# A fused two-block transformer kernel: weight slots with the low parts written in place, eight raw slots, and more modulation tiles on TensorE

## Chip, cores and metric

The kernel runs on one core of one Trainium2 chip. The metric is the device time of one execution in microseconds.

## What is computed

Two transformer blocks in a row, on 256 tokens of width 2048, all in float32. Cut to what matters here:

```
# block 1: adaptive norms, a Fourier mixer, an MLP of hidden width 8192
sh1, sc1, g1, sh2, sc2, g2 = split(silu(c) @ w_mod + b_mod, 6)     # w_mod: 2048 x 12288
h = rms_norm(x, g) * (1 + sc1) + sh1
y = real(fft2(h, tokens and groups of 256 features)) @ fnet_w_out
x = x + g1 * rms_norm(y);  x = x + g2 * rms_norm(relu(mod(x, sh2, sc2) @ w_mlp_in)**2 @ w_mlp_out)
# block 2: x -> w_in (12 groups of 512 columns: gated linear attention, forgetting attention,
#          attention to 256 memory tokens with keys and values mem @ w_mem_kv), gates, @ w_out
x = x + (o * gate) @ w_out;  x = x + relu(rms_norm(x) @ w_up)**2 @ w_down
```

All matrices are read once: 450 MB and more of weights in a run.

## The kernel before

The program is written out for each engine, with semaphores.

**Weights.** A weight chunk is 256 rows by 512 columns, 512 KB, in SBUF as 128 partitions by 1024 floats. A group is eight chunks (`CH`), 2048 rows of 512 columns. There are 688 chunks: 16 for the memory's keys and values (`G_MEM`), 32 for fnet_w_out (`G_FN`), 256 for each MLP, 96 for w_in (`G_WIN`), 32 for w_out. Float32 accuracy is reached with two fp32r parts: ScalarE copies `raw` to `wh` (high part, `hi`, L755), VectorE writes `wl = raw - wh` (low part, `lo`, L1054), and TensorE multiplies high by high, high by low and low by high. `wh` and `wl` have eight slots each, one for each chunk of a group; `raw` has four (`RAW`). `T_chunk` keeps weights stationary (L379 and L380 in the MLPs, L383 to L385 elsewhere), `N_chunk` the activations (L397 to L399).

**Modulation.** A modulation tile is 128 rows by 1024 columns of w_mod, also 512 KB and in the same `raw` slots. Each of the six vectors has 32. VectorE adds each tile, scaled by silu(c), into an accumulator (`gemv`, L1080, a chain along each half); the tiles in `PE_MOD` go to TensorE instead, as eight products with one column (`mod_chunk`, L436: 16 instructions in the trace). `mod_sum` (L448) then adds up the accumulator over partitions with more one-column products. The tiles of g2 use a slot of their own (`slot`), loaded by GpSimd's queue during the first MLP.

**Order.** All loads into `raw` are numbered in one line (`chunk_c`, `mod_c`), load cc goes to slot cc % RAW, and SyncE issues them in that order, each behind a wait that the slot's former content is used up: `raw_used`, incremented by `lo` for a weight chunk, by `gemv` or `mod_chunk` for a tile. The order is: 32 tiles of sc1; 16 chunks of w_mem_kv, each followed by two tiles of sh1; 32 tiles of g1 (while TensorE does the DFT); 32 chunks of fnet_w_out, each followed by a tile of sc2; 32 tiles of sh2; the first MLP; w_in; w_out; the second MLP.

Every engine runs its list in order. ScalarE's `hi` waits for the landing and for the multiplication of the chunk eight earlier (`chunk_used`), VectorE's `lo` for `hi`, TensorE for `lo`. On VectorE and ScalarE, `lo_run` and `hi_run` handle chunks 4 to 7 of a group and 0 to 3 of the next, and behind that stands the evacuation of the group's sums from PSUM (`ps`), in w_in also the steps of the attention: `lvl_post` and `lvl_pre` prepare a decay level (`qd`, `kd`, L1394), which TensorE multiplies in `att_level` (L626) between two chunks. In sh2, TensorE does tiles 3 and 5, then the transposes of the residual stream (L421, `SH2_TURN`), which wait for VectorE's `dg`, then the other tiles; the sums of its halves are the last thing before the MLP.

Of the kernel before, what the change touches and what calls it, by code (L numbers as in the profile page):

```python
# [34 lines left out]
P = 128  # L35
# [7 lines left out]
RAW = 4  # L43
# [5 lines left out]
PE_MOD = dict(sc1=(2, 8, 13, 18, 24), sh1=(), sc2=(), sh2=(3, 5, 20, 25))  # L49
# [12 lines left out]
def program(nc, x, c, w_mod, b_mod, norm_g, w_mlp_in, w_mlp_out, fnet_w_out, mem, attn_g, w_in, gla_w2, gla_b,  # L62
# [3 lines left out]
    with ctx:  # L66
# [10 lines left out]
        O_RAW, O_WH, O_WL = 0, 16 * KB, 48 * KB  # L77
# [17 lines left out]
        wl = at("wl", [P, CH, 2, GC], F32R, O_WL)  # L95
# [125 lines left out]
        def _(sp):  # L221
            def load(cc, view):

                s = cc % RAW
                if cc >= RAW:
                    sp.wait_ge(sem(f"raw_used{s}"), cc // RAW)
                sp.dma_start(raw_slot(s, view), view).then_inc(sem(f"raw_landed{s}"), 16)
# [30 lines left out]
            def ring_group(r0, view_of):  # L258

                for i in range(CH):  # L260
                    sp.wait_ge(sem(f"raw_used{i % RAW}"), r0 + i // RAW)
                    sp.dma_start(raw[:, i % RAW, :].rearrange("p (t n) -> p t n", t=2),
                                 view_of(i)).then_inc(sem(f"raw_landed{i % RAW}"), 16)

            def mlp_loads(G0, w1, w2_):
                r0 = (CH * G0 + C_OFF) // RAW
                with sp.Fori(0, QT) as q:
                    with sp.Fori(0, GQ) as g:
                        ring_group(r0 + 16 * q + 2 * g,
                                   lambda i: rows(w1)[:, 2 * i:2 * i + 2, bass.ds(q * D + g * GC, GC)])  # L270
                    with sp.Fori(0, GQ) as g:
                        ring_group(r0 + 8 + 16 * q + 2 * g,
                                   lambda i: rows(w2_)[:, bass.ds(q * KT + 2 * i, 2), bass.ds(g * GC, GC)])

            mlp_loads(G_ML1, w_mlp_in[0], w_mlp_out[0])
            for k, (name, off) in enumerate(WIN_GROUPS):
                ring_group((CH * (G_WIN + k) + C_OFF) // RAW,
                           lambda i: rows(w_in)[:, 2 * i:2 * i + 2, W_IN[name] + off:W_IN[name] + off + GC])
            with sp.Fori(0, GQ) as g:
                ring_group((CH * G_WO + C_OFF) // RAW + 2 * g,  # L280
                           lambda i: rows(w_out)[:, 2 * i:2 * i + 2, bass.ds(g * GC, GC)])
# [83 lines left out]
        def _(pe):  # L365
            mm = nc.tensor.matmul

            def T_chunk(G, i, wide, s, r):

                pe.wait_ge(sem(f"raw_used{s}"), r)  # L370
                par = G % 2
                for t in range(2):
                    kt = 2 * i + t
                    for j in range(4):
                        a, b = wh[:, i, t, j * P:(j + 1) * P], wl[:, i, t, j * P:(j + 1) * P]
# [12 lines left out]
            def N_chunk(G, i, act, wide, s, r):  # L388

                pe.wait_ge(sem(f"raw_used{s}"), r)  # L390
                par = G % 2
                for t in range(2):
                    kt = 2 * i + t
                    for half in range(HALVES):
                        o = ps[:, (4 if wide else 2) * par + half, :]
                        hi, lo = (act[:, kt, z, half * P:(half + 1) * P] for z in range(2))
                        mm(o, hi, wh[:, i, t, :], start=kt == 0, stop=False, skip_group_check=True)  # L397
                        mm(o, hi, wl[:, i, t, :], start=False, stop=False, skip_group_check=True)  # L398
                        last = mm(o, lo, wh[:, i, t, :], start=False, stop=kt == KT - 1, skip_group_check=True)  # L399
                last.then_inc(sem("chunk_used"), 1)  # L400
# [24 lines left out]

            for part in range(2):
                pe.wait_ge(sem(f"rows_in{part}"), 16 * ((N_ROWS + 1 - part) // 2))
            nc.tensor.transpose(ps[:, 0, 0:VROWS], vrow[0:VROWS, :], ident[0:VROWS, 0:VROWS]).then_inc(sem("vt_mm"), 1)

            def mod_chunk(vec, c0, n, bank, start=False):  # L430
# [7 lines left out]
                last.then_inc(sem(f"raw_used{s}"), 1)  # L438

            def mod_sum(vec, c0, a, bank, halves=(0, 1)):  # L440

                for half in halves:
                    n = [n for n in range(MODN) if mod_part(vec, n)[1] == half and n not in PE_MOD[vec]][-1]
                    s, r = slot_of(mod_c(c0, n))
                    pe.wait_ge(sem(f"raw_used{s}"), r)
# [14 lines left out]
            mod_sum("sc1", C_SC1, 0, 2)  # L460
            for i in range(CH):
                if i % 2 == 0:
                    pe.wait_ge(sem("xt_ready"), 1 + i // 2)
                T_chunk(G_MEM, i, False, *slot_of(chunk_c(i)))
            for i in range(CH):
                if i == 0:
                    pe.wait_ge(sem("mod_out"), 1)
                N_chunk(G_MEM + 1, i, xt, False, *slot_of(chunk_c(CH + i)))
# [53 lines left out]
            for n in (MODN - 2, MODN - 1):  # L522
                s, r = slot_of(mod_c(C_G1, n))
                pe.wait_ge(sem(f"raw_used{s}"), r)
            gate_rows(0, (4, 5, 6, 7))

            for g in range(GQ):
                bank_free(G_FN + g)
                for i in range(CH):
                    if g == 0:  # L530
                        pe.wait_ge(sem("fm_lo"), i + 1)
                    N_chunk(G_FN + g, i, xt, False, *slot_of(chunk_c(CH * (G_FN + g) + i)))
# [16 lines left out]
            def mlp(G0, build, ups, between=None):  # L549

                r0 = (CH * G0 + C_OFF) // RAW

                def down(q, p, e, last=False):
                    pe.wait_ge(sem("evacuated"), q * 8 + p * 2 + (G0 + 4 + e - 1))
                    for i in range(CH):
# [3 lines left out]
                        N_chunk(G0 + e, i, u, True, i % RAW, q * 16 + p * 4 + (r0 + 8 + 2 * e + i // RAW + 1))  # L559
# [3 lines left out]
                def quarter(q, last=False):  # L563
                    with pe.Fori(0, 2) as p:
                        for e in range(2):
                            pe.wait_ge(sem("evacuated"), q * 8 + p * 2 + (G0 + e - 1))
                            for i in range(CH):
                                if i % 2 == 0 and e == 0:
                                    pe.wait_ge(sem("xt_ready"), 4 * build + 1 + i // 2)
                                T_chunk(G0 + e, i, True, i % RAW, q * 16 + p * 4 + (r0 + 2 * e + i // RAW + 1))  # L570
# [109 lines left out]
            for k, (name, off) in enumerate(WIN_GROUPS):  # L680
                G = G_WIN + k
                bank_free(G)
                for i in range(CH):
                    if k == 0 and i % 2 == 0:
                        pe.wait_ge(sem("xt_ready"), 8 + i // 2 + 1)
                    sr = slot_of(CH * G + C_OFF + i)
# [41 lines left out]
            with pe.Fori(0, 2) as p:  # L728
                for e in range(2):
                    pe.wait_ge(sem("evacuated"), p * 2 + (G_WO + e - 1))  # L730
                    for i in range(CH):
                        if i % 2 == 0 and e == 0:
                            pe.wait_ge(sem("z_lo"), i // 2 + 1)
                        N_chunk(G_WO + e, i, u, False, i % RAW, p * 4 + ((CH * G_WO + C_OFF) // RAW + 2 * e + i // RAW + 1))
# [5 lines left out]
        def _(act):  # L740
# [20 lines left out]
            def hi_run(m0, between=None):  # L761

                for j in range(CH):
# [4 lines left out]
                    hi(i, (j % RAW, (m0 + (C_OFF + RAW * (j // RAW) + RAW)) * 4), m0 + (j - CH + 1))  # L768
# [128 lines left out]
            def mlp_quarter(G0, ups, q, last=False):  # L897
# [11 lines left out]
                def down(p, e, final=False):  # L909
                    m0 = q * 64 + p * 16 + (CH * (G0 + 4 + e) + 4)  # L910
                    if final:
                        for j in range(4):
                            hi(4 + j, (j % RAW, (m0 + (C_OFF + RAW)) * 4), m0 + (j - CH + 1))
# [127 lines left out]
        def _(dve):  # L1041
# [18 lines left out]
            def lo_run(m0, between=None):  # L1060
                for j in range(CH):
                    if between:
                        between(j)
                    lo((4 + j) % CH, j % RAW, m0 + (j + 1))
# [3 lines left out]
            def gemv(vec, c0, n, a):  # L1068
# [6 lines left out]
                if (vec, half) in summed:  # L1075
                    s0, r0 = summed[vec, half]
                    dve.wait_ge(sem(f"raw_used{s0}"), r0)
                summed[vec, half] = (s, r)
                t = (acc[0], acc[1], acc2)[a][:, half * MODC:(half + 1) * MODC]
                V.scalar_tensor_tensor(out=t, in0=raw[:, s, :], scalar=siluc[:, kt:kt + 1], in1=t,  # L1080
                                       op0=ALU.mult, op1=ALU.add).then_inc(sem(f"raw_used{s}"), 1)
# [197 lines left out]
            def mlp_quarter(G0, ups, q, side, onto, last=False):  # L1279
# [34 lines left out]
                def down(p, e, tail=False):  # L1314
# [4 lines left out]
                    if tail and not side:  # L1319
                        for j in range(4):  # L1320
                            lo(4 + j, j % RAW, m0 + (j + 1))
# [280 lines left out]
```

## Time and profile before

| | us |
|---|---|
| three timed runs | 2348.45 median (2344.02, 2348.45, 2353.89) |
| span of the profiled execution, first to last instruction | 2343.0 |
| TensorE (PE) busy | 2171.3 |
| VectorE (DVE) busy | 1401.3 |
| ScalarE (ACT) busy | 974.4 |
| GpSimd (POOL) busy | 47.4 |

The profiled execution has no time of its own beside its span; the timed runs are the nearest to it. PEld in the rows is TensorE's loading of weights, which overlaps its matmuls. Matmul durations overlap each other in the trace; the distance of two starts is the better measure of what one costs. PEclk is the granted clock as a share of 2.4 GHz, and takes the values 0.5 and 1.0 only, so a number between is a mean over time. The digits of the slices are busy shares in tenths of 58.6 us.

### The profile page before, as it was taken

What the parts mean: (1) busy time and instruction counts of PE and PEld (TensorE: products, weight loads), DVE (VectorE), ACT (ScalarE), POOL (GpSimd) and SP (SyncE); (2) the same over time, 40 slices, a digit from 0 to 9 for tenths busy, and PEclk for the clock granted to TensorE, in tenths of its full rate; (3) what the DMA queues carried; (4) which work ended last, traced back from release to release, by engine and by line L of the source; (5) the groups of instructions that cost most, each with busy time, mean ns of one, the idle gap of its engine ahead of it and who ended that gap; (6) DMA issues with size and microseconds to landing.
All of it is one profiled execution on the core that took longest, in us unless ns stands there. A gap on an engine that the chain in (4) does not pass through costs nothing.

```text
span 2343.0 us, 30666 instructions
## 1 busy us (share of the span) xinstructions
PE 2171.3 (93%) x11609; PEld 1859.2 (79%) x11609; DVE 1401.3 (60%) x1340; ACT 974.4 (42%) x1126; POOL 47.4 (2%) x68
## 2 busy tenths in 40 slices
PE   3688784999999999999799999998999999999999
PEld 3666564888888888888688888987888888888887
DVE  5779767665565565565566645655564564564553
ACT  3132332544444444344343355664343343443442
POOL 0000000000000000001000000000000000000000
PEclk7789995999999999999899998999999999999999
DMA  8988887676566566667364433464565555555554
GB/s 309 304 287 281 287 284 275 216 233 223 185 227 223 193 218 227 200 210 236 127 199 144 144 101 115 130 224 148 181 201 192 181 192 188 187 194 182 186 196 144
DMA packets 219173, 478.75 MB, mean 204 GB/s; under 512 B 14708, under 2 KB 15084, under 8 KB 218336
## 3 DMA queue, kind: packets, MB, share of 16 engines
q1 hardware_dynamic: 211940, 450.98, 57.8%
q0 software_dynamic: 6192, 24.64, 3.1%
q10 hardware_dynamic: 972, 2.19, 0.3%
q8 instruction: 46, 0.75, 0.1%
q14 instruction: 23, 0.19, 0.0%
HBM read 472.50 MB, written 5.24 MB: 204 GB/s over the span
## 4 chain that ended last, share of the span: by engine, by line
PE 74%; DMA 10%; DVE 10%; ACT 4%; issue 2%; SPq 0%; DVEq 0%; ACTq 0%
PE ps L379 21%; PE ps L397 11%; PE ps L398 11%; PE ps L399 11%; PE ps L380 10%; DMA raw<-in_fnet_w_out_dram 3%; DMA raw<-in_w_mod_dram 3%; DVE wl L1054 3%; DVE acc L1080 2%; PE ps L383 2%; PE ps L384 2%; PE ps L385 2%; ACT wh L755 2%; DMA raw<-in_w_mem_kv_dram 1%; DMA raw<-in_w_in_dram 1%
## 5 line engine op out<-in xcount | busy, mean ns | idle before, releaser
L1054 DVE TENSOR_TENSOR wl<-raw,wh 128x1024 fp32r<-128x1024 f32 x688 | 821.3, 1222 | 371.7 <-ACT wh L755 361.6
L755 ACT ACTIVATE wh<-raw 128x1024 fp32r<-128x1024 f32 x688 | 707.5, 1055 | 683.9 <-DMA raw<-in_w_down_dram 131.9
L379 PE MATMUL ps<-xt,wh 128*128 128x512 f32 x2048 | 724.3, 399 | 0.0
L380 PE MATMUL ps<-xt,wl 128*128 128x256 f32 x2048 | 575.8, 281 | 0.0
L379 PEld LDWEIGHTS ps<-xt,wh 128*128 128x128 f32 x2048 | 385.6, 188 | 94.7
L397 PE MATMUL ps<-wh,u 128*128 128x512 f32 x1152 | 449.0, 390 | 0.0
L398 PE MATMUL ps<-wl,u 128*128 128x512 f32 x1152 | 448.2, 389 | 0.0
L399 PE MATMUL ps<-wh,u 128*128 128x512 f32 x1152 | 448.2, 389 | 0.0
L380 PEld LDWEIGHTS ps<-xt,wl 128*128 128x128 f32 x2048 | 387.8, 189 | 0.2
L397 PEld LDWEIGHTS ps<-wh,u 128*128 128x128 f32 x1152 | 216.3, 188 | 45.6 <-DVE wl L1054 0.2
L399 PEld LDWEIGHTS ps<-wh,u 128*128 128x128 f32 x1152 | 216.3, 188 | 44.9
L398 PEld LDWEIGHTS ps<-wl,u 128*128 128x128 f32 x1152 | 216.3, 188 | 44.8 <-issue 0.5
L1080 DVE SCALAR_TENSOR_TENSOR acc<-raw,siluc,acc 128x1024 f32<-128x1024 f32 x151 | 190.1, 1280 | 26.8 <-DMA raw<-in_w_mod_dram 25.1
L383 PE MATMUL ps<-xt,wh 128*128 128x256 f32 x640 | 186.9, 292 | 8.5 <-DVE wl L1054 8.5
L384 PE MATMUL ps<-xt,wh 128*128 128x256 f32 x640 | 183.4, 287 | 0.0
L385 PE MATMUL ps<-xt,wl 128*128 128x256 f32 x640 | 183.2, 286 | 0.0
L397 PE MATMUL ps<-wh,xt 128*128 128x512 f32 x256 | 107.6, 420 | 30.7 <-DVE wl L1054 30.6
L1296 DVE TENSOR_TENSOR tmp<-ps,tmp 128x1024 f32<-128x1024 f32 x32 | 39.2, 1224 | 161.5 <-ACT tmp L905 161.5
L383 PEld LDWEIGHTS ps<-xt,wh 128*128 128x128 f32 x640 | 125.2, 196 | 11.8 <-DVE wl L1054 7.7
L384 PEld LDWEIGHTS ps<-xt,wh 128*128 128x128 f32 x640 | 125.2, 196 | 1.1 <-issue 1.0
L385 PEld LDWEIGHTS ps<-xt,wl 128*128 128x128 f32 x640 | 125.1, 195 | 0.0
L905 ACT ACTIVATE tmp<-ps 128x1024 f32<-128x1024 f32 x32 | 32.8, 1026 | 187.0 <-PE ps L380 187.0
(251 smaller groups left out, 1544.5 us busy)
## 6 DMA issues: line engine op xcount, KB each, us to landing
raw<-in_w_mod_dram SPq DMA_DIRECT2D x160, 512.0 KB, 5.0
raw<-in_w_mlp_in_dram SPq DMA_DIRECT2D x128, 512.0 KB, 4.6
raw<-in_w_mlp_out_dram SPq DMA_DIRECT2D x128, 512.0 KB, 5.2
raw<-in_w_up_dram SPq DMA_DIRECT2D x128, 512.0 KB, 4.5
raw<-in_w_down_dram SPq DMA_DIRECT2D x128, 512.0 KB, 5.5
raw<-in_w_in_dram SPq DMA_DIRECT2D x96, 512.0 KB, 4.7
raw<-in_fnet_w_out_dram SPq DMA_DIRECT2D x32, 512.0 KB, 5.2
slot<-in_w_mod_dram POOLq DMA_DIRECT2D x32, 512.0 KB, 4.9
```

Source lines behind the costliest of these rows:

```text
L379: mm(o, a, flat(xt[:, kt, :, :]), start=first, stop=end, skip_group_check=True)
L380: last = mm(o[:, 0:S], b, xt[:, kt, 0, :], start=False, stop=end, skip_group_check=True)
L383: mm(o, a, xt[:, kt, 0, :], start=first and j % 2 == 0, stop=False, skip_group_check=True)
L384: mm(o, a, xt[:, kt, 1, :], start=False, stop=False, skip_group_check=True)
L385: last = mm(o, b, xt[:, kt, 0, :], start=False, stop=end, skip_group_check=True)
L397: mm(o, hi, wh[:, i, t, :], start=kt == 0, stop=False, skip_group_check=True)
L398: mm(o, hi, wl[:, i, t, :], start=False, stop=False, skip_group_check=True)
L399: last = mm(o, lo, wh[:, i, t, :], start=False, stop=kt == KT - 1, skip_group_check=True)
L755: A(flat(wh[:, i, :, :]), raw[:, landed[0], :], ACT.Copy).then_inc(sem("w_hi"), 1)
L1054: V.tensor_tensor(flat(wl[:, i, :, :]), raw[:, s, :], flat(wh[:, i, :, :]).bitcast(F32), ALU.subtract).then_inc(sem(f"raw_used{s}"), 1)
L1080: V.scalar_tensor_tensor(out=t, in0=raw[:, s, :], scalar=siluc[:, kt:kt + 1], in1=t, op0=ALU.mult, op1=ALU.add).then_inc(sem(f"raw_used{s} ...
L1296: V.tensor_tensor(tmp[:, :, :], ps[:, b0:b0 + 4, 0:S], tmp[:, :, :], ALU.add).then_inc(sem("evacuated"), 1)
```

## The change

Three things.

1. `wl` has no memory of its own any more. It is a second name for the `raw` slots, with another type: `lo` writes the low part over the raw chunk that it reads, in the same slot.
2. `raw` has eight slots in place of four. A slot with a weight chunk is free when TensorE has multiplied the chunk (`chunk_used`), one with a modulation tile when the tile is used (`mod_used`). `w_lo` tells TensorE that a low part is there.
3. `PE_MOD` has 17 more tiles: ten of sc1 in place of five, six of sh1 in place of none, ten of sh2 in place of four. Those of sh1 are multiplied right behind the memory chunk that their loads follow. The load of x stays behind the fourth tile.

```diff
-RAW = 4
+RAW = 8
-PE_MOD = dict(sc1=(2, 8, 13, 18, 24), sh1=(), sc2=(), sh2=(3, 5, 20, 25))
+PE_MOD = dict(sc1=(2, 5, 8, 11, 13, 16, 18, 21, 24, 27), sh1=(3, 7, 11, 15, 19, 23), sc2=(), sh2=(3, 5, 8, 11, 14, 17, 20, 23, 25, 28))
-        O_RAW, O_WH, O_WL = 0, 16 * KB, 48 * KB
+        O_RAW, O_WH = 0, 32 * KB
-        wl = at("wl", [P, CH, 2, GC], F32R, O_WL)
+        wl = at("wl", [P, RAW, 2, GC], F32R, O_RAW)
...
+        CHUNK_AT = {chunk_c(m): m for m in range(CH * G_ML1)}
+        MOD_AT = sorted(mod_c(c0, n) for c0 in (C_SC1, C_MEM, C_G1, C_FN, C_SH2) for n in range(MODN))
+        MOD_USES = [sum(1 for cc in MOD_AT if cc % RAW == s) for s in range(RAW)]
+
+        def mod_used(cc):
+            return sem(f"mod_used{cc % RAW}"), sum(1 for o in MOD_AT if o % RAW == cc % RAW and o <= cc)
...
             def load(cc, view):
                 s = cc % RAW
-                if cc >= RAW:
-                    sp.wait_ge(sem(f"raw_used{s}"), cc // RAW)
+                if cc - RAW in CHUNK_AT:
+                    sp.wait_ge(sem("chunk_used"), CHUNK_AT[cc - RAW] + 1)
+                elif cc >= RAW:
+                    sp.wait_ge(*mod_used(cc - RAW))
...
             for n in range(MODN):
-                if n == RAW:
+                if n == 4:
                     sp.dma_start(h[:, :, :], x[0].rearrange("(a p) d -> p a d", p=P)).then_inc(sem("x_in"), 16)
...
-            def ring_group(r0, view_of):
+            def ring_group(m0, view_of, behind_mods=False):
                 for i in range(CH):
-                    sp.wait_ge(sem(f"raw_used{i % RAW}"), r0 + i // RAW)
+                    if behind_mods:
+                        sp.wait_ge(sem(f"mod_used{i}"), MOD_USES[i])
+                    sp.wait_ge(sem("chunk_used"), m0 + (i - RAW + 1))
...
-            def T_chunk(G, i, wide, s, r):
-                pe.wait_ge(sem(f"raw_used{s}"), r)
+            def T_chunk(G, i, wide, s, split):
+                pe.wait_ge(sem("w_lo"), split)
...
+            def sh1_chunks(m):
+                for n in (2 * m, 2 * m + 1):
+                    if n in PE_MOD["sh1"]:
+                        mod_chunk("sh1", C_MEM, n, 7, n == PE_MOD["sh1"][0])
...
             def lo(i, s, hi_value):
                 dve.wait_ge(sem("w_hi"), hi_value)
-                V.tensor_tensor(flat(wl[:, i, :, :]), raw[:, s, :], flat(wh[:, i, :, :]).bitcast(F32),
-                                ALU.subtract).then_inc(sem(f"raw_used{s}"), 1)
+                V.tensor_tensor(flat(wl[:, s, :, :]), raw[:, s, :], flat(wh[:, i, :, :]).bitcast(F32),
+                                ALU.subtract).then_inc(sem("w_lo"), 1)
```

`N_chunk` changes as `T_chunk` does, and the other waits on `raw_used` become waits on `mod_used` or `w_lo` with the matching counts.

## Rows read from the trace of the kernel before

**Rows 1.** Page: TensorE's total, and TensorE and DMA in 40 slices

```profile
PE 2171.3 (93%) x11609; PEld 1859.2 (79%) x11609; DVE 1401.3 (60%) x1340; ACT 974.4 (42%) x1126; POOL 47.4 (2%) x68
...
PE   3688784999999999999799999998999999999999
...
DMA  8988887676566566667364433464565555555554
```

**Rows 2.** Windows at the borders of the stages

```profile
core 0: us, PE busy (x) PEld busy (x) DVE busy (x) ACT busy (x) POOL busy (x), PEclk, DMA share, GB/s
10.00:20.00 10.00, 4.71 (x21) 4.49 (x22) 3.42 (x12) 5.69 (x7) 0.00 (x0) 1.00 1.03 419
20.00:73.40 53.40, 22.21 (x126) 21.47 (x126) 44.46 (x48) 15.19 (x24) 2.30 (x2) 0.63 0.86 295
73.40:156.20 82.80, 64.91 (x325) 55.55 (x326) 60.96 (x52) 23.42 (x22) 2.29 (x2) 0.85 0.92 307
156.20:228.70 72.50, 59.79 (x330) 50.73 (x328) 64.48 (x102) 19.87 (x51) 2.83 (x3) 0.91 0.78 263
228.70:346.80 118.10, 97.14 (x384) 72.45 (x385) 83.28 (x72) 36.65 (x43) 2.85 (x3) 0.97 0.85 289
346.80:411.80 65.00, 33.27 (x193) 32.69 (x192) 47.16 (x52) 19.53 (x41) 6.29 (x4) 0.61 0.79 275
350.00:356.00 6.00, 3.06 (x20) 2.98 (x20) 5.05 (x6) 4.28 (x8) 1.51 (x2) 0.60 0.08 27
411.80:1125.80 714.00, 714.00 (x3593) 604.97 (x3593) 429.89 (x367) 316.21 (x358) 22.35 (x39) 1.00 0.65 215
```

**Rows 3.** Chain of work in order of time, projection (start us, us, what)

```profile
228.57 5.46 DMA raw<-in_fnet_w_out_dram
...
234.06 1.06 ACT wh L755
...
235.15 1.24 DVE wl L1054
```

**Rows 4.** Timeline of TensorE: half-clock matmuls, then chunk 0 and chunk 1 of fnet_w_out

```profile
81.00 0.41 PE L383 MATMUL ps<-xt,wh 128*128 128x256 f32 x1
81.22 0.41 PE L384 MATMUL ps<-xt,wh 128*128 128x256 f32 x1
...
228.69 0.47 PE L397 MATMUL ps<-wh,xt 128*128 128x512 f32 x1 [0.35 <-DVE wl L1054]
...
231.50 0.41 PE L397 MATMUL ps<-wh,xt 128*128 128x512 f32 x1
```

**Rows 5.** Page, groups: VectorE's two operations (busy, mean ns, idle before)

```profile
L1054 DVE TENSOR_TENSOR wl<-raw,wh 128x1024 fp32r<-128x1024 f32 x688 | 821.3, 1222 | 371.7 <-ACT wh L755 361.6
...
L1080 DVE SCALAR_TENSOR_TENSOR acc<-raw,siluc,acc 128x1024 f32<-128x1024 f32 x151 | 190.1, 1280 | 26.8 <-DMA raw<-in_w_mod_dram 25.1
```

**Rows 6.** Timeline of TensorE: one-column products and the transposes

```profile
30.55 1.84 PE L436 MATMUL ps<-siluc,raw 128*128 128x1 f32 x16
...
73.40 6.96 PE L448 MATMUL ps<-ones,acc 128*128 128x1 f32 x32 [9.01 <-DVE acc L1080]
...
360.74 3.57 PE L436 MATMUL ps<-siluc,raw 128*128 128x1 f32 x16 [7.67 <-DMA raw<-in_w_mod_dram]
364.17 9.46 PE L421 MATMUL ps<-dg,h 128*128 128x128 f32 x64
```

**Rows 7.** Landing: one load by itself (chain), and w_down's median (page)

```profile
400.59 3.65 DMA raw<-in_w_mod_dram
...
raw<-in_w_down_dram SPq DMA_DIRECT2D x128, 512.0 KB, 5.5
```

**Rows 8.** Decay levels: waits of TensorE, its level at 1242, VectorE's last subtractions

```profile
PE ps L626 <- DVE kd L1394: 11.5, 4, 4.1
...
1242.00 2.16 PE L626 MATMUL ps<-qd,kd 64*128 64x128 f32 x32
...
1248.16 2.45 DVE L1054 TENSOR_TENSOR wl<-raw,wh 128x1024 fp32r<-128x1024 f32 x2 [0.17 <-ACT wh L755]
```

More of the change, by code:

```diff
@@ L256, in _ @@
                 load(C_SH2 + n, mod_view(3, 2 * (n % KT) + n // KT))
[L258 removed]
+            def ring_group(m0, view_of, behind_mods=False):
                 for i in range(CH):
[L261 to L263 removed]
+                    if behind_mods:
+                        sp.wait_ge(sem(f"mod_used{i}"), MOD_USES[i])
+                    sp.wait_ge(sem("chunk_used"), m0 + (i - RAW + 1))
+                    sp.dma_start(raw[:, i, :].rearrange("p (t n) -> p t n", t=2),
+                                 view_of(i)).then_inc(sem(f"raw_landed{i}"), 16)
             def mlp_loads(G0, w1, w2_):
[L266 removed]
                 with sp.Fori(0, QT) as q:
                     with sp.Fori(0, GQ) as g:
[L269 to L270 removed]
+                        ring_group(q * 64 + g * 8 + CH * G0,
+                                   lambda i: rows(w1)[:, 2 * i:2 * i + 2, bass.ds(q * D + g * GC, GC)], G0 == G_ML1)
                     with sp.Fori(0, GQ) as g:
[L272 removed]
+                        ring_group(q * 64 + g * 8 + CH * (G0 + 4),
                                    lambda i: rows(w2_)[:, bass.ds(q * KT + 2 * i, 2), bass.ds(g * GC, GC)])
@@ L386, in T_chunk, with N_chunk @@
                 last.then_inc(sem("chunk_used"), 1)
-            def N_chunk(G, i, act, wide, s, r):
-                pe.wait_ge(sem(f"raw_used{s}"), r)
+            def N_chunk(G, i, act, wide, s, split):
+                pe.wait_ge(sem("w_lo"), split)
                 par = G % 2
@@ L397, in N_chunk @@
                         mm(o, hi, wh[:, i, t, :], start=kt == 0, stop=False, skip_group_check=True)
-                        mm(o, hi, wl[:, i, t, :], start=False, stop=False, skip_group_check=True)
+                        mm(o, hi, wl[:, s, t, :], start=False, stop=False, skip_group_check=True)
                         last = mm(o, lo, wh[:, i, t, :], start=False, stop=kt == KT - 1, skip_group_check=True)
@@ L423, in transposes, with early @@
                     last.then_inc(sem("turned"), 1)
+            def early(m):
+                return chunk_c(m) % RAW, m + 1
             for part in range(2):
@@ L437, in mod_chunk @@
                               start=start and j == 0, stop=False, skip_group_check=True)
-                last.then_inc(sem(f"raw_used{s}"), 1)
+                last.then_inc(mod_used(mod_c(c0, n))[0], 1)
             def mod_sum(vec, c0, a, bank, halves=(0, 1)):
@@ L463, in _ @@
                     pe.wait_ge(sem("xt_ready"), 1 + i // 2)
-                T_chunk(G_MEM, i, False, *slot_of(chunk_c(i)))
+                T_chunk(G_MEM, i, False, *early(i))
+                sh1_chunks(i)
             for i in range(CH):
@@ L467, in _ @@
                     pe.wait_ge(sem("mod_out"), 1)
-                N_chunk(G_MEM + 1, i, xt, False, *slot_of(chunk_c(CH + i)))
+                N_chunk(G_MEM + 1, i, xt, False, *early(CH + i))
+                sh1_chunks(CH + i)
                 if i == 3:
@@ L531, in _ @@
                         pe.wait_ge(sem("fm_lo"), i + 1)
-                    N_chunk(G_FN + g, i, xt, False, *slot_of(chunk_c(CH * (G_FN + g) + i)))
+                    N_chunk(G_FN + g, i, xt, False, *early(CH * (G_FN + g) + i))
             pe.wait_ge(sem("slot_used"), 2)
@@ L1063, in lo_run @@
                         between(j)
[L1064 removed]
+                    lo((4 + j) % CH, (4 + j) % RAW, m0 + (j + 1))
             summed = {}
@@ L1075, in gemv @@
                 if (vec, half) in summed:
-                    s0, r0 = summed[vec, half]
-                    dve.wait_ge(sem(f"raw_used{s0}"), r0)
-                summed[vec, half] = (s, r)
+                    dve.wait_ge(*summed[vec, half])
+                summed[vec, half] = mod_used(mod_c(c0, n))
                 t = (acc[0], acc[1], acc2)[a][:, half * MODC:(half + 1) * MODC]
                 V.scalar_tensor_tensor(out=t, in0=raw[:, s, :], scalar=siluc[:, kt:kt + 1], in1=t,
-                                       op0=ALU.mult, op1=ALU.add).then_inc(sem(f"raw_used{s}"), 1)
+                                       op0=ALU.mult, op1=ALU.add).then_inc(mod_used(mod_c(c0, n))[0], 1)
             def mean(parts, n, done, value):
```

27 lines of the change are left out of this document (12 added, 15 removed).

## Prediction

> **What bounds the kernel now.** I read the page first [rows 1]: TensorE is busy 93% of a 2343.0 us span, but its digits are 3 to 8 in the first seven slices and 9 nearly everywhere after, while the DMA digits are 7 to 9 in just those first seven. So the kernel has two parts with different limits. Cut at the borders of the code's stages [rows 2], TensorE has no idle time from 411.8 to 1125.8 us (first MLP), at 1.00 of its clock. Before that nothing is full: TensorE is busy 42 to 82% of the five stages, VectorE 71 to 89%, the DMA engines' share is 0.78 to 0.92.
>
> What ends the waits there is read in the chain of the fnet projection [rows 3]: a load of 5.46 us, ScalarE's copy of 1.06, VectorE's subtraction of 1.24, and then the next load, which could not be issued before. That is four slots running dry: 7.8 us for two pairs of loads (weight and modulation tile), 3.9 us a pair, and the stage's 118.1 us over 32 pairs are 3.69. Latency sets this stage, not bandwidth: 289 GB/s at a share of 0.85 is 340 at a full one. Next in line are VectorE with 83.3 us busy and TensorE with 97.1 (this counts overlapping ends: by start times a chunk takes 2.81 us [rows 4], 32 of them 90).
>
> **The change, stage by stage.** Eight loads can be out instead of four; but a weight slot is free only when TensorE has multiplied it, as its low part lies in it. ScalarE's and VectorE's instructions for a chunk stay (1.06 us, and 1222 ns [rows 5]), writing in place included; I cost that at nothing, since reads and writes are as many (10% more would be 688 x 0.12 = 83 us of VectorE time, hidden where TensorE leads, and on the path for some 3 us in stage 4). SP issues in program order, so each wait for a weight slot also holds the modulation loads behind it. The 17 tiles leave VectorE at 1280 ns each, 21.8 us, and cost TensorE 16 instructions each: 1.84 us at the full clock, 3.57 at half [rows 6], 31 to 61 us, all before 411.8.
>
> Stage 1, scale vector, to the sum at 73.4 us. Loads no longer wait for four slots. From 20 to 73.4 us 15.75 MB moved; at a full share that is 53.4 x 0.86 = 45.9 us, 7.5 less. VectorE had 44.5 us busy and loses 5 x 1.28, TensorE had 22.2 and gains 5 x 3.57, to 40.1; both fit. I take 7 us, nearer to that end because the loads never wait for a multiplication of weights here. Bounds: 3.5 (share 0.92, as in stage 2) and 8 (stage 5's rate, 275 / 0.79 = 348 GB/s).
>
> Stage 2, memory keys and values, to 156.2. The DMA side could give 82.8 x 0.08 = 6.6 us. TensorE was 64.9 us busy and gets six tiles, 11 to 21.4 us: 76 to 86 of 82.8. A third of the loads hold their slots some 5 us longer, until TensorE is through. So most is eaten: I take 1 us. Bounds: 5 won; and if the clock stays at half throughout, 16 chunks at 24 x 0.213 = 5.1 us [rows 4] + 6 x 3.57 + the sum's 7 = 110 us, 27 lost.
>
> At this place a rule speaks for the change. The row first: the 6.96 us of one-column products at 73.4 ran without a gap, and at 0.50 of the clock, 1.2 GHz, to their end; the tile at 360.74 took 3.57, at the same level [rows 6]. The Trainium skill, "TensorE: Matmul & The Clock Gate", Part 1, says that the throttled state is the default and that activity releases it. Taken plainly, a TensorE filled with modulation tiles would speed itself up; the trace has not shown that, and the sum goes by 3.57.
>
> Stage 3, DFT, to 228.7. VectorE is busy 64.5 of 72.5 us and none of its tiles here is moved: 0, bounds 0 and 3.
>
> Stage 4, projection with the second scale vector. Eight slots hold four chunks when TensorE is free, at 228.34, so chunk 0 is done at 231.1. Its slot is chunk 4's: 3.65 us for a load that comes alone [rows 7], 234.7. From there to chunk 31 are 27 pairs of 1.049 MB. At a share of 0.96, 326 GB/s, they take 3.22 us each, 87 us; then 1.06 + 1.24 + 2.81: 326.8, against 346.8. A slot's loop, 3.65 + 1.06 + 1.24 + 2.81 = 8.8 us for four pairs, no longer sets the pace. TensorE's floor is 228.3 + 90 = 318; VectorE's 83.3 us end at 312. Gain 20 us; bounds 15 (stage 2's 307 GB/s: 3.42 a pair) and 28 (TensorE's floor).
>
> The first loads moved 419 GB/s for 10 us [rows 2]. "DMA: Bandwidth & Descriptors", Specifications, in the Trainium skill gives some 358 GB/s as HBM's limit for a core; the trace does not agree. By that figure a pair would take 2.93 us and this stage give 27.
>
> Stage 5, shift vector, to the MLP at 411.8. From 350 to 356 us, while VectorE does the residual, DMA stood nearly still, share 0.08 [rows 2]; eight slots fetch four more tiles there, 6 us. Tile 5, which came at 360.74 for want of a slot, held the transposes to 364.17 [rows 6]; early, it gives them up to 3.4 us. But then eight tiles and two sums of 3.5 follow on TensorE at half clock. From the stage's start: transposes 14 to 23.4, copies out some 1.6 later (estimate: 1024 columns were 1.06), then 8 x 3.57 + 2 x 3.5 = 35.6: 60.6, where the MLP began at 65. Gain 4; bounds 0, and 9 at the full clock, where DMA leads.
>
> Input projections. TensorE waits four times, 11.5 us, for VectorE's decay level [rows 8], the longest at 1256.6. There VectorE's eighth subtraction ends at 1250.6, as its load could go out only when the fourth was through. Now it goes out when TensorE has done the old chunk 3, at 1242.0: 1242.0 + 3.65 + 1.06 + 1.24 = 1248. So 2.6 of 4.1 us go and 1.5 stay; if 1.4 stay of each, 6 us are won. Bounds 0 (a load of 5.5, as in a burst, leaves 0.8) and 12 (all).
>
> MLPs: 0. Loads are needed 19 us after they can go out, and their landing, 5.5 us [rows 7], lies beside TensorE's work in both kernels.
>
> Sum: 7 + 1 + 0 + 20 + 4 + 6 = 38 us, made against the span of 2343.0. The three timed runs (2344.02 to 2353.89) have their median 5 us above it; I take those 5 us as unchanged: 2348.45 - 38 = 2310.
>
> **Rivals.**
> TensorE takes VectorE's place: it falls to half clock in stages 1, 2 and 5 and stays there. Stage 2 loses 15 (between its ends, as three quarters of it would run slow) instead of winning 1; stages 1 and 5 give 4, projection and levels 26: 2348 - 15 = 2333. For it: clock 0.63, 0.85 and 0.61 in these stages; against: stage 2's chunks stand denser than before, and 0.85 was reached with gaps. 0.13.
>
> The depth buys nothing: DMA stays at 289 to 307 GB/s, a longer queue being only a longer landing. Then stage 4 gives its four prefetched loads, 7 us, the levels 3: 2338. Against: a share of 1.03 in the first loads, 0.92 in stage 2. 0.09.
>
> More: stage 4 at TensorE's floor (28), stages 1 and 5 with tiles at 1.84 us (8 + 9), stage 2 its 5, all level waits (12): 62 us, 2286. For it: tile 8 at 30.55 did take 1.84; against: it stood behind dense work. 0.05. Both pages named above point this way, the clock gate's rule and the DMA limit's 27 us; no term here is from them.
>
> Slower: the wide MLP groups. A load there starts only behind TensorE. VectorE ends a group's subtractions at 11.2 (fourth chunk used) + 5.5 + 2.3 = 19 us, the group ends at 22.5, and its evacuation can slip some 3.7 us more before the next group's fifth chunk is late. So if landing took over 5.5 + 3.5 + 3.7 = 12.7 us, each of 64 groups would stall by the excess: 1 us more is 64 us, 2348 - 38 + 64 = 2374. Against: landings under half of that, at a DMA share of 0.65. 0.05.
>
> **How the numbers follow.** The forecast has 0.68, its own range 2296 to 2325. The range 2292 to 2335 takes in most of the first rival and leaves out the others, 2 in 10. With 10 us between timed runs, 0.5% (12 us; 2336.7) is about what can be told. Faster: 0.68 + 0.05 + 0.11 of the first rival = 0.84; same: its rest and the second, 0.11; slower 0.05.
>
> **What would show it.** First memory chunk on TensorE near 73 us instead of 80.3; first DFT matmul near 148 instead of 156.2; a pair every 3.2 us in the projection, DMA share 0.95, its last matmul 28 us earlier; shift tiles back to back on TensorE; level waits of 1 to 2 us; both MLPs as long as before. The prediction is wrong if the clock of stage 2 is under 0.7, the DMA share of stage 4 stays at 0.85, or TensorE has gaps in an MLP.

## The result, and the profile after

| | before | after |
|---|---|---|
| median of four timed runs, us | 2351.17 (2344.02 to 2356.05) | 2286.34 (2285.20 to 2287.13) |
| span of the profiled execution, us | 2343.0 | 2284.5 |
| TensorE busy, us | 2171.3 | 2199.5 |
| VectorE busy, us | 1401.3 | 1370.7 |

The ratio of the times is 0.972, with a 95% interval of 0.970 to 0.974: faster, by 64.8 us. The forecast was 2310 and its range began at 2292, so the direction was right and the size too small: the kernel gained 1.7 times what was forecast. The time is that of the rival called "more" (2286), which had a chance of 0.05; how far that is its mechanism, and how far luck, is said below.

The page of the kernel after: its totals, TensorE's digits, granted clock and DMA share in 40 slices, and the groups that answer to [rows 1, 5].

```profile
PE 2199.5 (96%) x11881; PEld 1897.3 (83%) x11881; DVE 1370.7 (60%) x1323; ACT 968.1 (42%) x1126; POOL 47.4 (2%) x68
...
PE   6888999999999999999899999998999999999999
...
PEclk8899987999999999999899989999999999999999
DMA  9888988667666767767465535664666666666664
...
L1073 DVE TENSOR_TENSOR wl<-raw,wh 128x1024 fp32r<-128x1024 f32 x688 | 813.2, 1222 | 358.8 <-ACT wh L774 357.6
...
L1098 DVE SCALAR_TENSOR_TENSOR acc<-raw,siluc,acc 128x1024 f32<-128x1024 f32 x134 | 168.0, 1278 | 15.7 <-DMA raw<-in_w_mod_dram 14.0
```

The first six slices have 6 to 9 for TensorE where [rows 1] has 3 to 8. The subtraction costs 1222 ns, written in place or not.

The kernel after in windows at the borders of the same stages, for [rows 2]; the last but one is again 350 to 356 us.

```profile
core 0: us, PE busy (x) PEld busy (x) DVE busy (x) ACT busy (x) POOL busy (x), PEclk, DMA share, GB/s
10.00:20.00 10.00, 4.52 (x20) 4.30 (x21) 3.26 (x12) 5.69 (x7) 0.00 (x0) 1.00 1.03 420
20.00:65.10 45.10, 35.72 (x207) 34.97 (x206) 38.51 (x43) 16.15 (x25) 2.30 (x2) 0.74 1.00 379
65.10:143.30 78.20, 70.74 (x420) 63.03 (x421) 53.74 (x47) 22.53 (x22) 2.29 (x2) 0.89 0.89 324
143.30:215.80 72.50, 59.75 (x330) 50.98 (x329) 64.17 (x101) 21.58 (x52) 2.83 (x3) 0.90 0.80 274
215.80:308.70 92.90, 89.73 (x384) 72.64 (x384) 81.63 (x72) 34.57 (x41) 2.85 (x3) 0.98 0.96 355
308.70:366.00 57.30, 52.11 (x287) 51.68 (x286) 39.53 (x46) 19.52 (x41) 6.29 (x4) 0.61 0.81 302
350.00:356.00 6.00, 6.00 (x30) 6.00 (x30) 5.79 (x8) 0.00 (x0) 0.00 (x0) 0.50 0.98 365
366.00:1078.00 712.00, 712.00 (x3583) 603.06 (x3583) 424.96 (x366) 313.88 (x358) 22.35 (x39) 1.00 0.69 214
```

Read beside [rows 2]: stage 1 runs at 379 GB/s instead of 295, and the projection at 355 instead of 289. In the projection TensorE is busy 89.7 of 92.9 us: it is TensorE's stage now, no longer the loads'. The first MLP has no gap in either kernel.

Cut at the same instructions (the sum's first product, the first product of the DFT, of the projection, its end, the MLP, the transposes after it, those after w_out), the time went as follows. Each column is one trace. The last two columns are from experiments below: the new slots with the old tiles, and the new tiles with the old slots.

| stage | before | forecast gain | after | gain | slots alone | tiles alone |
|---|---|---|---|---|---|---|
| 1 scale vector, to the sum | 73.4 | 7 | 65.1 | 8.3 | 65.7 | 78.2 |
| 2 memory, first shift vector | 82.8 | 1 | 78.2 | 4.6 | 82.5 | 103.6 |
| 3 DFT | 72.2 | 0 | 72.5 | -0.3 | 72.6 | 72.0 |
| 4 projection | 118.5 | 20 | 93.0 | 25.5 | 94.7 | 119.7 |
| 5 second shift vector | 65.0 | 4 | 57.8 | 7.2 | 56.4 | 75.4 |
| first MLP | 727.6 | 0 | 726.8 | 0.8 | 727.6 | 729.7 |
| w_in, attention, w_out | 478.5 | 6 | 464.9 | 13.6 | 465.8 | 483.0 |
| second MLP | 725.1 | 0 | 726.4 | -1.3 | 723.5 | 725.7 |
| span | 2343.0 | 38 | 2284.5 | 58.5 | 2288.7 | 2387.3 |

The spans differ by 58.5 us, the medians by 64.8. The profiled execution of after took 2286.12 us, 1.6 more than its span, and every other profiled run here lies 1.6 to 2.1 above its own. The profiled execution of before, with its span of 2343.0, was thus one of its shortest; the kernel before scatters over 12 us, the one after over 2, and over 4 with its repetition below (`again`).

### The profile page after: what moved, and what is told of

It is laid out like the page before. It is cut to its first block, busy times and chain, and to the rows that moved or that the text cites. A ratio compares the mean times of both kernels' runs of the same rounds, so it can differ in the third digit from the quotient of the medians.

```text
span 2284.5 us, 31892 instructions
## 1 busy us (share of the span) xinstructions
PE 2199.5 (96%) x11881; PEld 1897.3 (83%) x11881; DVE 1370.7 (60%) x1323; ACT 968.1 (42%) x1126; POOL 47.4 (2%) x68
## 4 chain that ended last, share of the span: by engine, by line
PE 86%; DVE 5%; DMA 5%; ACT 2%; issue 2%; SPq 0%; DVEq 0%; ACTq 0%
PE ps L390 21%; PE ps L408 13%; PE ps L410 13%; PE ps L409 13%; PE ps L391 11%; PE ps L394 3%; PE ps L396 3%; PE ps L395 3%; DVE acc L1098 1%; DMA raw<-in_w_mod_dram 1%; PE ps L432 1%; DMA raw<-in_w_mem_kv_dram 1%; PE ps L451 1%; DMA raw<-in_w_in_dram 1%; DVE wl L1073 1%
## 5 line engine op out<-in xcount | busy, mean ns | idle before, releaser
L1073 DVE TENSOR_TENSOR wl<-raw,wh 128x1024 fp32r<-128x1024 f32 x688 | 813.2, 1222 | 358.8 <-ACT wh L774 357.6
L1098 DVE SCALAR_TENSOR_TENSOR acc<-raw,siluc,acc 128x1024 f32<-128x1024 f32 x134 | 168.0, 1278 | 15.7 <-DMA raw<-in_w_mod_dram 14.0
```

Source lines behind the costliest of these rows:

```text
L1073: V.tensor_tensor(flat(wl[:, s, :, :]), raw[:, s, :], flat(wh[:, i, :, :]).bitcast(F32), ALU.subtract).then_inc(sem("w_lo"), 1)
```

## The experiments

Twelve runs: ten kernels, and two of the kernels repeated. They were measured in three groups, with the kernel before beside each: 2352.51 (2341.38 to 2353.99) for runs 1 to 4, 2349.33 (2342.31 to 2350.42) for 5 to 8, 2351.54 (2343.37 to 2353.75) for 9 to 12. Ratios are to the kernel before of the same group. The theory at the outset: the slots carry nearly the whole gain, because a slot was held while its content was copied, subtracted and summed; the tiles are worth little. The rivals: the moved tiles carry part of it; or it is a deeper queue of loads as such.

### 1. `rate`: loads alone, by the number in flight

The kernel leaves out all computation; its output is x. It runs 24 loads for each number in flight, of modulation tiles, of weight chunks, and of both in turn.

```python
def segment(kind, depth, loads=24):
    first = done[0]
    for n in range(loads):
        o = done[0] - depth
        if o >= first:
            sp.wait_ge(sem(f"landed{o % RAW}"), 16 * (o // RAW + 1))
...
for kind in (0, 1, 2):
    for depth in (1, 2, 3, 4, 6, 8):
        segment(kind, depth)
```

> Loads alone, nothing is computed (the output is x): 24 loads of 512 KB at each depth of 1, 2, 3, 4, 6 and 8 in flight, first modulation tiles (4 KB rows), then weight chunks (2 KB rows), then the two in turn. Theory: the rate grows with the depth, some 145 GB/s at 1, 330 to 345 at 4, and 370 to 380 at 8, and the engines' busy share is near 1 already at 4, so that share is no linear measure of the room left. Rival: the rate is flat at 340 from depth 3 or 4 on, and the changed kernel's 355 to 379 GB/s come from something else (which rows are fetched, fewer pauses).

It took 899.1 us, in its one timed execution. Windows inside the segments (POOL, PEclk, DMA share, GB/s): tiles with 1, 2, 3, 4, 6 and 8 in flight, then both kinds in turn with 2, 3 and 4.

```profile
10.00:80.00 70.00, 0.00 (x0) 1.00 0.49 148
92.00:136.00 44.00, 0.00 (x0) 1.00 0.75 237
146.00:180.00 34.00, 0.00 (x0) 1.00 0.93 319
188.00:214.00 26.00, 0.00 (x0) 1.00 1.02 404
221.00:247.00 26.00, 0.00 (x0) 1.00 1.02 404
255.00:281.00 26.00, 0.00 (x0) 1.00 1.02 405
...
680.00:720.00 40.00, 0.00 (x0) 1.00 0.74 234
735.00:768.00 33.00, 0.00 (x0) 1.00 0.88 290
778.00:805.00 27.00, 0.00 (x0) 1.00 1.02 387
```

Four in flight are as good as eight. The expectation had both rates too low (330 to 345 at four, 370 to 380 at eight), and that the rate is flat from four on is the rival's shape, though at 404 GB/s and not at 340. And the share is no measure of the rate that is left: at 0.88 it was 290 GB/s, which by proportion would be 330 at a full share, and it was 387. With three in flight the alternating loads give 290, and the projection of the kernel before ran at 289. That fits the number it had in flight: of its loads, 64 in 118.1 us, each took some 5.1 us to land, 64 x 5.1 / 118.1 = 2.8. After: 64 loads, 6.0 and 5.2 us, 3.9 in flight.

### 2. `slots_only`: the new slots, the old tiles

```diff
-PE_MOD = dict(sc1=(2, 5, 8, 11, 13, 16, 18, 21, 24, 27), sh1=(3, 7, 11, 15, 19, 23), sc2=(), sh2=(3, 5, 8, 11, 14, 17, 20, 23, 25, 28))
+PE_MOD = dict(sc1=(2, 8, 13, 18, 24), sh1=(), sc2=(), sh2=(3, 5, 20, 25))
```

> The changed kernel with the old choice of tiles for TensorE (9 in place of 26). Theory: slots carry nearly all: 2290 to 2300 us, 55 us off, with the shift vector's stage some 5 us shorter than in the changed kernel and the first two stages 3 to 8 longer. Rival (the tiles matter as much): 2310 us or more.

Measured 2287.83 us (2286.17 to 2290.40), ratio 0.9735 (0.9706 to 0.9763). The slots alone give the gain; the tiles' share, 1.5 us of the medians, is within the scatter. It came out a little lower than the 2290 to 2300 expected. The first two stages are 4.9 us longer than after, as expected, but stage 5 is only 1.4 us shorter and not 5.

### 3. `tiles_only`: the old slots, the new tiles

The kernel before with the new `PE_MOD` and `sh1_chunks`.

> The kernel before with the new choice of tiles, four slots and separate low parts. Theory: with four slots VectorE is not what limits the first stages, so the tiles win nothing, 2340 to 2360 us, and may lose where TensorE's half-clock tiles hold one of only four slots. Rival: 20 us or more are won by relieving VectorE.

Measured 2387.26 us (2380.80 to 2388.97), ratio 1.0151 (1.0118 to 1.0184): 35 us slower than before by the medians, and slower than the 2340 to 2360 expected; 44 by the spans, of which stage 2 has 21, stage 5 10 and stage 1 5. Its windows in stages 1 and 2:

```profile
20.00:78.20 58.20, 37.84 (x208) 36.98 (x207) 39.32 (x43) 15.18 (x24) 2.30 (x2) 0.71 0.80 267
78.20:181.80 103.60, 81.28 (x421) 72.21 (x422) 53.68 (x46) 22.89 (x22) 2.29 (x2) 0.78 0.73 248
```

No engine is full and the rate falls to 248 GB/s: a tile behind a chunk on TensorE keeps its slot until TensorE is through with that chunk, and with four slots the next loads wait for it. The waits of the queue that issues the loads (SyncE, SPq) show it. In stage 2 it waits six times, once for each moved tile, and before had no such wait; in after, with eight slots, the same six waits are 5.1 us. `tiles_only`, then after:

```profile
SPq L227 <- PE ps L436: 34.4, 6, 6.5
```

```profile
SPq L237 <- PE ps L451: 5.1, 6, 0.9
```

### 4. `proj_four`: four slots in the projection only

```diff
             def load(cc, view):
+                if C_FN <= cc < C_SH2:
+                    o = cc - 4
+                    if o in CHUNK_AT:
+                        sp.wait_ge(sem("w_lo"), CHUNK_AT[o] + 1)
+                    elif o >= 0:
+                        sp.wait_ge(*mod_used(o))
```

> The changed kernel, but in the projection stage a load also waits until the item four before it is used (low part made, or tile added), as with four slots. Theory: this stage returns from 92.9 us to 113 to 118, the kernel to 2286 + 22 = 2308 us, DMA back to 290 GB/s. Rival: the stage stays under 105 us, as the gain came from the relief elsewhere.

Measured 2314.32 us (2309.18 to 2317.74), ratio 0.9855 (0.9824 to 0.9885). The window of its projection:

```profile
215.80:334.10 118.30, 98.44 (x385) 73.55 (x384) 82.43 (x72) 36.66 (x43) 2.85 (x3) 0.96 0.87 295
```

That is the window of before in [rows 2], 118.1 us and 289 GB/s, in a kernel that is otherwise the one after, low parts written in place included. The stage's gain is the slots' alone, 25.4 us. The kernel is 28 us slower than after by the medians, where 22 were expected.

### 5. `again`: the changed kernel once more

> The changed kernel once more, unchanged, as the measure for the three beside it. 2285 to 2288 us.

Measured 2286.01 us (2284.01 to 2288.06), ratio 0.9733 (0.9713 to 0.9754), span 2286.4. Stage by stage it repeats after within 1.1 us, but for stage 3, which took 75.8 instead of 72.5. Single stages before the MLP are therefore good to some 3 us, and stage 2 to less: `mix` and `mix_again` below are one kernel, and have 80.5 and 75.0 us there.

### 6. `mix`: six tiles of sh2 on TensorE in place of ten

```diff
-PE_MOD = dict(..., sh2=(3, 5, 8, 11, 14, 17, 20, 23, 25, 28))
+PE_MOD = dict(..., sh2=(3, 5, 18, 21, 24, 27))
```

> The changed kernel with other tiles of the shift vector on TensorE: 3, 5, 18, 21, 24, 27, so none between the transposes and the sum of the first half. Theory: in the changed kernel TensorE sets stage 5 (52.1 of 57.3 us busy, tiles 8, 11 and 14 come late and hold slots of later loads), with slots alone VectorE does (56.4 us); a balance between the two gives some 52 us, the kernel 2281. Rival: DMA or the residual's chain sets the stage, and it stays at 56 to 58 us.

Measured 2282.89 us (2277.02 to 2286.26), ratio 0.9714 (0.9690 to 0.9739). Stage 5 takes 53.2 us instead of 57.8. TensorE in stage 5, after and then `mix`:

```profile
323.05 9.86 PE L432 MATMUL ps<-dg,h 128*128 128x128 f32 x64 [2.63 <-DVE dg L1112]
334.57 7.11 PE L451 MATMUL ps<-siluc,raw 128*128 128x1 f32 x48 [1.66 <-ACT x1t L900]
341.54 3.55 PE L462 MATMUL ps<-ones,acc 128*128 128x1 f32 x16
344.96 17.21 PE L451 MATMUL ps<-siluc,raw 128*128 128x1 f32 x80
363.07 3.57 PE L462 MATMUL ps<-ones,acc 128*128 128x1 f32 x16 [0.91 <-DVE acc L1098]
```

```profile
325.52 10.37 PE L432 MATMUL ps<-dg,h 128*128 128x128 f32 x64 [3.60 <-DVE dg L1112]
340.60 3.54 PE L462 MATMUL ps<-ones,acc 128*128 128x1 f32 x16 [4.71 <-DVE acc L1098]
344.00 13.79 PE L451 MATMUL ps<-siluc,raw 128*128 128x1 f32 x64
361.00 3.58 PE L462 MATMUL ps<-ones,acc 128*128 128x1 f32 x16 [3.20 <-DVE acc L1098]
```

After has eight tiles and two sums in one piece behind the transposes, as the forecast had it, and TensorE is the bound. With six tiles TensorE waits 4.7 and 3.2 us for VectorE's accumulator, and the stage is shorter still. What the surplus tiles do to VectorE stands in its timeline of after:

```profile
333.37 1.28 DVE L1098 SCALAR_TENSOR_TENSOR acc<-raw,siluc,acc 128x1024 f32<-128x1024 f32 x1 [0.94 <-DMA raw<-in_w_mod_dram]
340.20 1.28 DVE L1098 SCALAR_TENSOR_TENSOR acc<-raw,siluc,acc 128x1024 f32<-128x1024 f32 x1 [5.54 <-DMA raw<-in_w_mod_dram]
```

It waits 5.54 us for a load. I read that as a load held behind a slot whose tile TensorE reaches only at 334.57; no run takes this wait away by itself. The waits of SyncE's queue from 320 to 342 us of after fit, and `mix` has none on a tile of TensorE from 320 to 345 us:

```profile
SPq L237 <- PE ps L451: 11.8, 3, 9.3
```

### 7. `sh1_none`: no tile of the first shift vector on TensorE

```diff
-PE_MOD = dict(..., sh1=(3, 7, 11, 15, 19, 23), ...)
+PE_MOD = dict(..., sh1=(), ...)
```

> The changed kernel without tiles of sh1 on TensorE. Theory: the six tiles are what shortened stage 2 (82.5 us with slots alone, 78.2 with them), by relieving VectorE, whose wait list stands before each low part: stage 2 back at 82 to 83, kernel +4, 2290 us. Rival: the difference of the two traces was chance or came from stage 1, and stage 2 stays at 78.

Measured 2287.59 us (2283.76 to 2290.66), ratio 0.9741 (0.9717 to 0.9764). Stage 2 took 74.3 us, less than after's 78.2 and not more, as I had expected; stage 3 took 77.5 instead of 72.5, and stage 5, which has not changed, 61 instead of 57.8. Stage 2 alone decides nothing: with the six tiles it took 75.0 to 80.5 us in the other traces with eight slots there, without them 74.3 here, 77.0 in `mix_sh1_none` and 82.5 in `slots_only`. What stands is the whole kernel, 1.3 to 1.6 us slower by the medians, within the scatter: no gain of the six tiles can be measured. The expectation of a stage 2 of 82 to 83 us fell; that of the kernel, 2290, was 2.4 us too high.

### 8. `levels_four`: four slots in w_in only

```diff
-            def ring_group(m0, view_of, behind_mods=False):
+            def ring_group(m0, view_of, behind_mods=False, four=False):
...
+                    if four:
+                        sp.wait_ge(sem("w_lo"), m0 + (i - 4 + 1))
```

> The changed kernel, but a w_in load also waits until the low part of the chunk four before it is made, as with four slots. Theory: the 14 us that w_in's stage won between the second and third transposes (478.5 to 464.9 us) come from these loads leaving earlier: back to 475 to 478, kernel 2298. Rival: they come from TensorE's clock by chance, and nothing changes.

Measured 2301.50 us (2296.67 to 2302.09), ratio 0.9796 (0.9773 to 0.9818): 15.5 us slower than `again` beside it, and 3.5 more than the 2298 expected. w_in to w_out takes 480.0 us, before's 478.5. TensorE's waits for the decay levels in that part, after and then `levels_four`, for the first of [rows 8]:

```profile
PE ps L645 <- DVE kd L1412: 5.3, 4, 1.7
```

```profile
PE ps L647 <- DVE kd L1414: 11.6, 4, 4.2
```

Windows over the decay levels, of before, after and `levels_four` in this order:

```profile
1214.90:1338.00 123.10, 111.62 (x817) 100.74 (x816) 78.47 (x73) 40.15 (x40) 0.00 (x0) 0.96 0.43 141
```

```profile
1169.90:1282.40 112.50, 107.21 (x817) 96.71 (x816) 77.00 (x73) 39.19 (x39) 0.00 (x0) 1.00 0.53 150
```

```profile
1169.50:1292.90 123.40, 111.82 (x817) 100.83 (x816) 78.56 (x73) 39.77 (x39) 0.00 (x0) 0.96 0.46 138
```

The waits shrink by 6.2 us, as forecast. But the same 817 matmuls are also busy 4.4 us less, and the granted clock is 1.00 instead of 0.96: without the longer pauses it did not fall. 6.2 + 4.4 = 10.6 us, which is 123.1 - 112.5. `levels_four` brings both back, so the clock follows the loads here and not chance. Before spent two stretches of this part at half clock, and the first begins inside the longest wait, the 4.1 us that ended at 1256.62, the second right behind one of 2.8 us; `levels_four` has two of the same lengths, after none:

```profile
1255.70:1262.50 6.80, 5.88 (x37) 5.27 (x38) 0.86 (x2) 0.00 (x0) 0.00 (x0) 0.50 0.01 2
1289.90:1293.30 3.40, 3.40 (x32) 3.38 (x32) 0.00 (x0) 0.00 (x0) 0.00 (x0) 0.50 0.02 5
```

### 9. `flight4`: eight slots, four loads in flight

```diff
             def load(cc, view):
+                if 0 <= cc < C_ML1:
+                    o = cc - 4
+                    if o >= 0:
+                        sp.wait_ge(sem(f"raw_landed{o % RAW}"), 16 * (o // RAW + 1))
```

> The changed kernel with one more wait ahead of each load up to the end of the shift vector's tiles: load number n goes out only when load n - 4 has landed. Eight slots stay, but at most four loads are in flight. Theory: what the old kernel lacked was not more than four loads in flight (four saturated the DMA in the run of loads alone, 404 and 387 GB/s), but slots for loads while others are being split and multiplied. Then this kernel is as fast as the changed one: span 2284 to 2290, projection stage 93 to 95 us, ratio to before 0.971 to 0.977. Rival, that more than four in flight carries the gain: projection stage back toward 110 us or more, span 2305 to 2325, ratio 0.985 or more.

The limit of four holds up to the last tile ahead of the first MLP; from there on the loads are as in after.

Measured 2291.08 us (2284.57 to 2292.29), ratio 0.9752 (0.9733 to 0.9771), span 2282.9; the projection took 94.5 us at 346 GB/s. Three of its four runs are some 5 us above after's, so a cost of a few us is possible; some nine tenths of the gain stay. What before lacked in these stages was not loads beyond four in flight, but slots for four loads while other slots are in use.

### 10. `first_four`: four slots in stages 1 and 2, new tiles

The rule of `proj_four` for the loads before `C_G1`.

> The changed kernel, but in stages 1 and 2 (scale vector, memory keys and values with the first shift vector) a load waits as if there were four slots: until the content of the load four places before it is used up. The 17 tiles stay on TensorE. Theory: the tiles only pay once slots are no longer short. With four slots a shift tile on TensorE holds its slot until the chunk ahead of it is multiplied, so stages 1 and 2 go back to the values of the kernel with tiles alone: stage 1 to 78 us (from 65), stage 2 to 100 us or more (from 78), some 35 us in all, span 2315 to 2322, ratio about 0.988. Rival, that the stages' gain in the changed kernel is mostly TensorE's new share of tiles: stages 1 and 2 at most 8 us longer than in the changed kernel, span 2285 to 2293.

Measured 2325.54 us (2323.11 to 2329.90), ratio 0.9893 (0.9873 to 0.9913). Stage 1 took 78.5 us and stage 2 103.3, as in `tiles_only` (78.2 and 103.6). The tiles on TensorE cost 26 us in these stages as long as slots are short, and nothing that can be measured once they are not. The expected span was 2315 to 2322; the median span of its four executions is 2323.9.

### 11 and 12. `mix_sh1_none` and `mix_again`

Six tiles of sh2 as in `mix`, without those of sh1; and `mix` unchanged.

> The changed kernel with ten scale tiles on TensorE as in it, but none of the first shift vector and six of the second (3, 5, 18, 21, 24, 27). Theory: the 17 moved tiles are worth about nothing, and a balanced set wins a few us where VectorE and TensorE are both near the loads' pace. Sum by stages of the two kernels it combines: stages 1 to 3 215 us, projection 93, shift vector 53, the rest 1918: span 2281 to 2285, ratio 0.970 to 0.973, not to be told from the kernel with six second shift tiles alone. Rival, that TensorE's tiles in stage 2 pay by keeping its clock up: 3 to 8 us slower than that kernel.

> The kernel with six second shift tiles (3, 5, 18, 21, 24, 27) once more, the first six shift tiles as in the changed kernel. If its lead of 3 us on the changed kernel was real, it gives a time of 2281 to 2285 again, with a shift stage of 53 us against 57; if it was scatter, 2286 to 2289.

Measured 2283.75 us (2282.00 to 2286.17), ratio 0.9718 (0.9701 to 0.9736), and 2283.66 us (2280.65 to 2285.48), ratio 0.9716 (0.9699 to 0.9733). Stage 5 took 53.6 and 53.2 us. The three runs with six tiles of sh2 have medians of 2282.9 to 2283.8, the two runs of the changed kernel 2286.0 and 2286.3. The intervals of the ratios overlap, so the 3 us are not established as a time; the 4 us in stage 5 are better founded: the three traces with six tiles have 53 to 54 us there, six of the seven eight-slot traces with ten tiles 57 to 58, and the seventh (`sh1_none`) 61.

## Why the prediction was too small

**What held.** The mechanism did: too few loads in flight, and not the bandwidth, set the stages before the MLP, and slots cure it (`slots_only`, `proj_four`). In the spans the sum said 38 us and the kernel gave 58.5. What failed is the size of the terms, of two above all: the input projections, 6 us where 13.6 came, and stage 4, 20 us where 25.5 came. The MLPs stayed as long as they were, and the subtraction in place costs nothing. No stall of late loads came up. Stage 1 won 8.3 us for 7 (its upper bound was 8).

**Stage 4, 25.5 us for 20: the rate was extrapolated by the share.** "At a share of 0.96, 326 GB/s, they take 3.22 us each, 87 us." That took 340 GB/s as the rate at a full share. The share does not grow in proportion to the rate: in `rate` 0.93 was 319 GB/s and 1.02 was 404. The stage could have 387; it took 355, at which a pair of 1.049 MB is 2.95 us, and its pace is TensorE's, which is busy 89.7 of 92.9 us and waits 3.0 us for the subtraction. It ended 2.5 us short of the bound named "TensorE's floor". That floor was itself a little high: it took 2.81 us a chunk [rows 4], and in the trace of after most matmuls here start 0.23 us apart, some 2.7 us a chunk. The chain through the stage shows what is left: its longest link is neither a weight nor a tile, but GpSimd's load of a row of norm_g, behind which VectorE's subtraction and TensorE stood.

```profile
218.59 4.31 DMA raw<-in_fnet_w_out_dram
...
227.88 7.24 DMA slot<-in_norm_g_dram
...
236.47 1.24 DVE wl L1073
```

The number of loads in flight should have been worked out instead, as above: 2.8 before. The row for a better rate was there, 419 GB/s in the first 10 us [rows 2], and was set aside. The figure of the Trainium skill cited in the prediction, 358 GB/s for a core, does not bind here, as `rate` has 404 (and 2.93 us a pair would have given 28 us for the stage, not 27). The Trainium skill, "HBM Reference", Specifications (TRN2), says also that a core streaming alone measures about 425 GB/s. This case's 404 with one queue and 420 in the first 10 us lie near it, and I had cited the other number.

**Projections of w_in, 13.6 us for 6: the largest miss.** The waits fell by 6.2 us, as worked out. The term put at nothing what a wait costs besides: 4.4 us by the clock in the levels, and some 4.1 more between 1338.0 and the end of w_out (279.87 us before, 275.73 after), less 1.1 us lost ahead of the levels. `levels_four` gives 15.1 us back, so all of it hangs on the loads of w_in; by what path the 4.1 us come was not traced.

**Stage 2, 4.6 us for 1.** The stage is too scattered to size this miss well, but two sizes were off. The moved tiles ran at the full clock, 1.84 us and not 3.57, between chunks:

```profile
88.09 1.84 PE L451 MATMUL ps<-siluc,raw 128*128 128x1 f32 x16
```

And the clock over the stage rose from 0.85 to 0.89. The first rival, in which TensorE falls to half clock for good, did not come; but stage 2 is no longer than 74.3 us without the tiles (`sh1_none`), and up to 82.5 (`slots_only`), so no help of theirs can be measured. The 4.6 us are two single traces, of a stage in which one kernel scatters by 5.5 us.

**Stage 5, 7.2 us for 4.** The term was worked out as TensorE's path of eight tiles and two sums: 35.6 us behind the transposes. The rows of after have it from 334.57 to the MLP's first product at 366.5, 31.9 us: the three tiles right behind the transposes took 7.11 us, 2.4 each, and only the five later ones 17.21, 3.4 each, the half-clock price that the term gave to all. And tile 5 was out of the transposes' way. The tiles themselves were no gain: with four of them (`slots_only`) the stage takes 56.4, with six 53.2, with ten 57.8.

**The base.** "I take those 5 us as unchanged": 1.6 of them were the constant difference of time and span, the rest a profiled execution on the fast side. After scatters less, and the 3 to 6 us became gain. In the spans 20.5 us are missing from the forecast: stage 4 has 5.5, w_in to w_out 7.6, stage 2 3.6, stage 5 3.2, stage 1 1.3, and the rest -0.8. Why before scatters by 12 us stays open; beside runs 1 to 4 its span was 2351.2 at a granted clock of 0.955 and 2339.7 at 0.960, so the clock goes with it.

**The chances.** Faster, with 0.84, came true. "More" had 0.05, because I priced it as several bounds met together. I now think that they have a common cause, and that once loads are not held back each stage goes to its next limit; that is an argument, not a measurement. Its number, 2286, was met partly by luck: its sum was 62 us where the spans gave 58.5, it had all 11.5 us of level waits gone where 5.3 stayed, its late shift tiles at 1.84 us where the last five took 3.4, and the rest is the shift of the base.

## What to carry to other kernels

Work out how many loads are really in flight (loads times landing time over the stage's time) before you believe a DMA share: here 2.8 of four slots were loading, 290 GB/s, and four would have been 387. Count the slots for what holds them besides the load, and do not extrapolate the rate by the share; look for the next engine's floor and expect the stage to reach it. Moving work to another engine did not pay here, since it did not free what was short: 17 tiles on TensorE cost 35 us with four slots and gave nothing measurable with eight.

## What the runs showed of the hardware

The rate of 512 KB loads of one queue by the number in flight: 148, 237, 319 and 404 GB/s for one to four with 4 KB rows, 137, 226, 283 and 389 with 2 KB rows (windows 300 to 365, 382 to 426, 440 to 472 and 484 to 510 us of `rate`; shifting them moves the lower three by some 3%), and no more from six or eight. The busy share with 4 KB rows was 0.49, 0.75, 0.93 and 1.02.

TensorE's clock in stage 5: from 341.6 to 362.1 us TensorE was busy with one-column products without a gap, and the granted clock was 0.50 throughout, 1.2 GHz; it had been higher just before, 0.76 on average from 334.6 to 341.5, and fell while TensorE was busy; its last wait before that was the 1.66 us up to 334.57. Two windows of after:

```profile
334.60:341.50 6.90, 6.90 (x48) 6.90 (x49) 1.34 (x2) 0.00 (x0) 0.00 (x0) 0.76 0.55 191
341.60:362.10 20.50, 20.50 (x97) 20.48 (x96) 15.09 (x19) 3.30 (x8) 0.00 (x0) 0.50 1.01 383
```

The same tiles took 1.84 us, at 2.4 GHz, between chunks of 256 and 512 columns in stage 2. The Trainium skill, "TensorE: Matmul & The Clock Gate", Part 1, says that activity releases the throttle; these 20.5 us of such activity did not.

A pause can cost more than its length: 6.2 us fewer of waits in the decay levels came with 4.4 us less of busy time for the same 817 matmuls, and `levels_four`, with the waits back, has the busy time back too (111.8 us against 107.2).
